# The sample's cross-attention scores of two heads, issued together in two column groups

## The reference

```python
def cross_attention(x, mem_k, mem_v, wq, wo):
    B, T, _ = x.shape
    q = (x @ wq).reshape(B, T, MEM_HEADS, MEM_HEAD_DIM)        # 4 heads of 512
    k = mem_k.reshape(B, -1, MEM_HEADS, MEM_HEAD_DIM)
    v = mem_v.reshape(B, -1, MEM_HEADS, MEM_HEAD_DIM)
    s = jnp.einsum('bqhd,bkhd->bhqk', q, k).astype(F32) * (MEM_HEAD_DIM ** -0.5)
    p = jax.nn.softmax(s, axis=-1).astype(x.dtype)
    o = jnp.einsum('bhqk,bkhd->bqhd', p, v).reshape(B, T, D_MODEL)
    return o @ wo
```

## Time and profile before

| | |
|---|---|
| time, median of 3 runs | 3115.37 us (3115.36 to 3124.46) |
| span of the profiled execution, first to last instruction | 3119.3 us; the page gives no other time of it |
| PE busy | 3036.5 us, 97% |
| DVE busy | 1907.7 us, 61% |
| ACT busy | 413.1 us, 13% |
| mean granted clock of TensorE | 0.987 |
| cross-attention stage, layer 0, layer 1 | 57.68 us, 56.70 us |

### The profile page before, as it was taken

The page is one execution under the profiler, slowest core; times in us unless marked ns, Lnnn a source line. Parts: engine busy times, 40 slices in busy tenths (PEclk is TensorE's granted clock), DMA queues, the critical chain, the costliest instruction groups (busy, mean ns, idle before and its releaser), DMA issues.

```text
span 3119.3 us, 47921 instructions
## 1 busy us (share of the span) xinstructions
PE 3036.5 (97%) x20530; PEld 2862.2 (92%) x20530; DVE 1907.7 (61%) x1485; ACT 413.1 (13%) x763; POOL 92.4 (3%) x64
## 2 busy tenths in 40 slices
PE   8999999899999999999999998999999999999998
PEld 6888899689989899999999996898999999999997
DVE  5666667646635766555565668744676555566565
ACT  2000003310220211000110003311031100011001
POOL 0000000100000000000000001000000000000000
PEclk9999999889999999999999999999999999999999
DMA  6666654234344355555555552453445555555542
GB/s 240 223 218 212 225 179 109 99 111 158 126 144 135 120 163 161 164 168 166 162 161 162 161 166 78 152 162 122 148 135 161 163 167 167 161 163 162 163 160 71
DMA packets 432693, 489.03 MB, mean 157 GB/s; under 512 B 16802, under 2 KB 388280, under 8 KB 431224
## 3 DMA queue, kind: packets, MB, share of 16 engines
q1 hardware_dynamic: 421344, 453.01, 46.0%
q0 software_dynamic: 4432, 18.15, 1.7%
q10 hardware_dynamic: 6836, 16.73, 1.5%
HBM read 476.47 MB, written 11.40 MB: 156 GB/s over the span
## 4 chain that ended last, share of the span: by engine, by line
PE 90%; DVE 7%; ACT 1%; DMA 1%; issue 1%; DVEq 0%; ACTq 0%
PE ps L217 24%; PE ps L219 24%; PE ps L218 24%; PE ps L370 4%; PE ps L371 4%; PE ps L372 4%; DVE WL L1336 2%; DVE X L1575 1%; PE ps L433 1%; PE ps L713 1%; PE ps L689 1%; DVE XL L1570 1%; DVE WH L1334 1%; PE ps L585 1%; PE ps L680 0%
## 5 line engine op out<-in xcount | busy, mean ns | idle before, releaser
L217 PE MATMUL ps<-XH,WH 128*128 128x288 f32 x3760 | 1117.3, 297 | 27.6 <-DVE XL L1341 11.8
L219 PE MATMUL ps<-XH,WL 128*128 128x288 f32 x3760 | 1111.5, 296 | 0.0
L218 PE MATMUL ps<-XL,WH 128*128 128x288 f32 x3760 | 1111.0, 295 | 0.0
L1334 DVE CAST WH<-RAW 128x2048 fp32r<-128x2048 f32 x433 | 535.5, 1237 | 837.6 <-PE ps L219 718.3
L1336 DVE TENSOR_TENSOR WL<-RAW,WH 128x2048 fp32r<-128x2048 f32 x433 | 1020.8, 2358 | 14.9
L217 PEld LDWEIGHTS ps<-XH,WH 128*128 128x128 f32 x3760 | 708.1, 188 | 37.0 <-issue 16.7
L218 PEld LDWEIGHTS ps<-XL,WH 128*128 128x128 f32 x3760 | 708.3, 188 | 0.2
L219 PEld LDWEIGHTS ps<-XH,WL 128*128 128x128 f32 x3760 | 708.3, 188 | 0.0
L217 PE MATMUL ps<-HH,WH 128*128 128x288 f32 x2048 | 604.7, 295 | 1.7 <-DVE WL L1336 1.7
L219 PE MATMUL ps<-HH,WL 128*128 128x288 f32 x2048 | 604.3, 295 | 0.0
L218 PE MATMUL ps<-HL,WH 128*128 128x288 f32 x2048 | 603.9, 295 | 0.0
(11 more groups left out here) (252 smaller groups left out, 1514.1 us busy)
## 6 DMA issues: line engine op xcount, KB each, us to landing
RAW<-in_mlp_up SPq DMA_DIRECT2D x128, 1024.0 KB, 5.4
RAW<-in_mlp_down SPq DMA_DIRECT2D x128, 1024.0 KB, 5.3
RAW<-in_xa_wk SPq DMA_DIRECT2D x32, 1024.0 KB, 5.1
RAW<-in_xa_wv SPq DMA_DIRECT2D x32, 1024.0 KB, 5.1
RAW<-in_xa_wq SPq DMA_DIRECT2D x32, 1024.0 KB, 5.4
RAW<-in_xa_wo SPq DMA_DIRECT2D x32, 1024.0 KB, 5.3
RAW<-in_w_in SPq DMA_DIRECT2D x22, 1024.0 KB, 5.3
RAW<-in_w_out SPq DMA_DIRECT2D x16, 1024.0 KB, 5.3
```

Source lines behind the costliest of these rows:

```text
L217: nc.tensor.matmul(out, wh, xh, start=start, stop=False)
L218: nc.tensor.matmul(out, wh, xl, start=False, stop=False)
L219: return nc.tensor.matmul(out, wl, xh, start=False, stop=stop)
L1334: V.tensor_copy(WH[:, h, :], RAW[:, s, :]).then_inc(split_hi, 1)
```

## The change

The sample's scores are no longer issued in each `scores(h)`. `scores(1)` issues those of heads 0 and 1, and `scores(3)` those of heads 2 and 3: for each of the four contraction tiles first the matmul of the one head, then that of the other, so that the column group alternates. ACT's copy of head 2's first key tile waits for scores(1), where it waited for scores(0), since KT[0] is read later. Number and shape of the matmuls stay.

Beside this, 31 semaphore names of the input stage and of the mixer are merged into five counters. The counts to wait for become the old ones plus what stands ahead in the group.

```diff
+    SIGNALS = {
+        "dve_inputs": (("memT_low", 8), ("xT_low", 16), ("conv", 32), ("sp_abs", 1), ("sp_done", 1), ("rec_ratio", 1)),
...
+        "pe_latents": (("stateT", 1), ("swap", 2), ("k_mm", 7), ("v_mm", 7), ("cacheT", 1)),
+    }
+    SIGNAL_OF = {n: (group, sum(c for _, c in of[:at])) for group, of in SIGNALS.items()
+                 for at, (n, _) in enumerate(of)}
+
     def sem(name):
+        if name in SIGNAL_OF:
+            name = SIGNAL_OF[name][0]
...
     def reached(name, n):
 
+        if name in SIGNAL_OF:
+            return sem(name), n + SIGNAL_OF[name][1]
...
-        pe.wait_ge(sem("xT_low"), NK)
+        pe.wait_ge(*reached("xT_low", NK))
...
-                def sample():
+                if h % 2:
                     for k in range(4):
-                        last = nc.tensor.matmul(ps[32 * h:32 * h + 32, 6, 0:256], QX[:, 4 * h + k, TP:T],
-                                                kt[:, k, 256:512], start=k == 0, stop=k == 3)
-                    return last
-
-                sample_last = sample()
+                        for hh in (h - 1, h):
+                            last = nc.tensor.matmul(ps[32 * hh:32 * hh + 32, 6, 0:256], QX[:, 4 * hh + k, TP:T],
+                                                    KT[hh % 2][:, k, 256:512], start=k == 0, stop=k == 3)
                 if h == 3:
-                    sample_last.then_inc(sem(f"{x}_s"), 1)
+                    last.then_inc(sem(f"{x}_s"), 1)
...
-                A(XH[:, k, :], ps[:, 4 + k % 4, 0:T], ACT.Copy).then_inc(sem("xT_high"), 1)
+                A(XH[:, k, :], ps[:, 4 + k % 4, 0:T], ACT.Copy)
...
                     if h >= 2 and k == 0:
-                        act.wait_ge(*reached(f"{x}_s", h - 1))
+                        act.wait_ge(*reached(f"{x}_s", 2))
```

More of the change, by code:

```diff
@@ L176, in build @@
     KIND_OF = {n: kind for kind, (names, _) in KINDS.items() for n in names}
+    SIGNALS = {
+        "dve_inputs": (("memT_low", 8), ("xT_low", 16), ("conv", 32), ("sp_abs", 1), ("sp_done", 1), ("rec_ratio", 1)),
+        "dve_latents": (("cq_n", 4), ("cq_low", 1), ("scanned", 1), ("ck_zero", 1), ("ck_n", 4), ("ck_low", 1),
+                        ("roped", 3)),
+        "act_gates": (("sp_exp", 1), ("cq_out0", 1), ("gates_sig", 16), ("tanh", 8), ("decay", 8), ("cq_out1", 1),
+                      ("sq_q", 1), ("rec_root", 1), ("ckv_out", 1)),
+        "pe_inputs": (("memT", 8), ("parT", 1), ("xT", 16), ("gate_mm", 16)),
+        "pe_latents": (("stateT", 1), ("swap", 2), ("k_mm", 7), ("v_mm", 7), ("cacheT", 1)),
+    }
+    SIGNAL_OF = {n: (group, sum(c for _, c in of[:at])) for group, of in SIGNALS.items()
+                 for at, (n, _) in enumerate(of)}
     def sem(name):
+        if name in SIGNAL_OF:
+            name = SIGNAL_OF[name][0]
         which, _, what = name.rpartition("_")
@@ L323, in mem_tiles @@
                 if r >= 4:
-                    pe.wait_ge(sem("memT_low"), r - 3)
+                    pe.wait_ge(*reached("memT_low", r - 3))
                 for k in range(2):
@@ L330, in mem_tiles @@
             pe.wait_ge(sem("par_in"), 16 * 12)
-            pe.wait_ge(sem("memT_low"), 8)
+            pe.wait_ge(*reached("memT_low", 8))
             for t, rows in enumerate((96, 96, 118)):
@@ L343, in x_tiles @@
                 if k >= 4:
-                    pe.wait_ge(sem("xT_low"), k - 3)
+                    pe.wait_ge(*reached("xT_low", k - 3))
                 for t, rows in enumerate((128, 128, 32)):
@@ L465, in _ @@
         pe.wait_ge(sem("gates_in"), 32)
-        pe.wait_ge(sem("conv"), 4 * LT)
+        pe.wait_ge(*reached("conv", 4 * LT))
         for n in range(2 * LT):
             if n >= 4:
-                pe.wait_ge(sem("gates_sig"), n - 3)
+                pe.wait_ge(*reached("gates_sig", n - 3))
             nc.tensor.matmul(ps[:, 4 + n % 4, 0:CW], GW[:, n, :], UC[:, n % LT, 0:CW], start=True,
@@ L473, in _ @@
         c0 = PHASES["ckv"]
-        pe.wait_ge(sem("cq_out0"), 1)
+        pe.wait_ge(*reached("cq_out0", 1))
         for q in range(2):
@@ L478, in _ @@
                       q == 0, q == 1).then_inc(chunk_used, 1)
-        pe.wait_ge(sem("gates_sig"), 2 * LT)
+        pe.wait_ge(*reached("gates_sig", 2 * LT))
         pe.wait_ge(sem("ones"), 1)
-        pe.wait_ge(sem("sq_q"), 1)
+        pe.wait_ge(*reached("sq_q", 1))
         for k in range(4):
@@ L486, in _ @@
         c0 = PHASES["kpe"]
-        pe.wait_ge(sem("cq_out1"), 1)
+        pe.wait_ge(*reached("cq_out1", 1))
         pe.wait_ge(chunk_split, c0 + 1)
@@ L505, in _ @@
         c0 = PHASES["uq"]
-        pe.wait_ge(sem("cq_low"), 1)
+        pe.wait_ge(*reached("cq_low", 1))
         pe.wait_ge(sem("kpe_out"), 1)
@@ L538, in _ @@
         pe.wait_ge(chunk_split, c0 + 1)
-        pe.wait_ge(sem("ck_low"), 1)
+        pe.wait_ge(*reached("ck_low", 1))
         for n in range(HEADS):
@@ L565, in _ @@
         pe.wait_ge(sem("v_out"), 8)
-        pe.wait_ge(sem("roped"), 3)
+        pe.wait_ge(*reached("roped", 3))
         for t, (c, rows) in enumerate(((0, 128), (128, 128), (384, 32))):
@@ L856, in _ @@
         for r in range(8):
-            act.wait_ge(sem("memT"), r + 1)
+            act.wait_ge(*reached("memT", r + 1))
             A(MTH[:, 2 * r:2 * r + 2, :].rearrange("p k n -> p (k n)"), ps[:, 4 + r % 4, :], ACT.Copy
               ).then_inc(sem("memT_high"), 1)
-        act.wait_ge(sem("parT"), 1)
+        act.wait_ge(*reached("parT", 1))
         for t, (n, c) in enumerate(((96, 0), (96, 96), (118, 192))):
@@ L911, in _ @@
         for n in range(2 * LT):
-            act.wait_ge(sem("gate_mm"), n + 1)
+            act.wait_ge(*reached("gate_mm", n + 1))
             m = n % LT
@@ L915, in _ @@
               bias=col((P_GAB if n < LT else P_GXB) + m)).then_inc(sem("gates_sig"), 1)
-        act.wait_ge(sem("gates_sig"), 2 * LT)
-        act.wait_ge(sem("sp_done"), 1)
+        act.wait_ge(*reached("gates_sig", 2 * LT))
+        act.wait_ge(*reached("sp_done", 1))
         act.wait_ge(sem("state_cols"), 2)
@@ L927, in _ @@
         A(CQ[:, 2:4, :], ps[:, 2:4, 0:T], ACT.Copy).then_inc(sem("cq_out1"), 1)
-        act.wait_ge(sem("cq_out0"), 1)
-        act.wait_ge(sem("cq_out1"), 1)
+        act.wait_ge(*reached("cq_out0", 1))
+        act.wait_ge(*reached("cq_out1", 1))
         A(SQM[:, :, :], CQ[:, :, :], ACT.Square).then_inc(sem("sq_q"), 1)
-        act.wait_ge(sem("rec_ratio"), 1)
+        act.wait_ge(*reached("rec_ratio", 1))
         A(TT[:, :, :], TT[:, :, :], ACT.Sqrt).then_inc(sem("rec_root"), 1)
@@ L960, in _ @@
         act.wait_ge(sem("pastT_out"), 2)
-        act.wait_ge(sem("ck_n"), 4)
+        act.wait_ge(*reached("ck_n", 4))
         A(CKH[:, :, :], CKT[:, :, :], ACT.Copy).then_inc(sem("ck_high"), 1)
@@ L968, in _ @@
         queries_out(3)
-        act.wait_ge(sem("stateT"), 1)
+        act.wait_ge(*reached("stateT", 1))
         A(SMALL[0:64, 128:256], ps[0:64, 7, 0:P], ACT.Copy).then_inc(sem("stateT_out"), 1)
@@ L976, in _ @@
             act.dma_start(dst, SMALL[r:r + n, 128:256]).then_inc(sem("stored"), 16)
-        act.wait_ge(sem("scanned"), 1)
+        act.wait_ge(*reached("scanned", 1))
         for n in range(HEADS):
             if n < HEADS - 1:
-                act.wait_ge(sem("k_mm"), n + 1)
+                act.wait_ge(*reached("k_mm", n + 1))
             else:
@@ L985, in _ @@
             if n < 7:
-                act.wait_ge(sem("v_mm"), n + 1)
+                act.wait_ge(*reached("v_mm", n + 1))
             else:
@@ L1212, in _ @@
         G.memset(RMS_EPS_COL, RMS_EPS).then_inc(sem("ones"), 1)
-        pool.wait_ge(sem("xT"), NK)
+        pool.wait_ge(*reached("xT", NK))
         pool.wait_ge(sem("par_done"), 1)
@@ L1401, in _ @@
         split(PHASES["cq"], 4)
-        dve.wait_ge(sem("decay"), LT)
+        dve.wait_ge(*reached("decay", LT))
         dve.wait_ge(sem("gated"), 1)
@@ L1430, in _ @@
         last.then_inc(sem("scanned"), 1)
-        dve.wait_ge(sem("scanned"), 1)
+        dve.wait_ge(*reached("scanned", 1))
         V.memset(CKT[:, :, KEYS:512], 0.0).then_inc(sem("ck_zero"), 1)
@@ L1445, in _ @@
         dve.wait_ge(sem("tables_in"), 16)
-        dve.wait_ge(sem("swap"), 2)
+        dve.wait_ge(*reached("swap", 2))
         bc = lambda x, n: x.unsqueeze(1).broadcast_to([P, n, T])
```

24 lines of the change are left out of this document (12 added, 12 removed).

## The result

The changed kernel takes 3126.39 us (median of 20 runs, 3122.94 to 3127.05), the kernel before 3116.82 us (20 runs, 3113.71 to 3130.7). The ratio, worked out from all runs of both, is 1.0023 (some 7 us), with a 95% interval of 1.0015 to 1.003; the two medians lie 9.6 us apart. So the change makes the kernel slower, where 3107.5 us and a range of 3103 to 3115 us were predicted. The 0.3% bound of the prediction (9.3 us) isn't crossed by the ratio, the range is missed by 11 us.

The account below looks back on a forecast made before the run. PE was taken as the bound, busy 97% of the span. Per layer 3.98 - 2 x 0.015 = 3.95 us, twice 7.9 us, off the median of 3115.37 us gave 3107.5 us; range 3103 to 3115 us.

Parts of the forecast that it names:

- The 0.3% bound of the prediction: Whole kernel: a measurement can tell about 0.3%, 9.3 us, from no change.
- Part 1: Cross-attention stages: removing the sample groups of heads 0 and 2 with their shape changes saves 3.98 us a layer.
- rival A: Sample scores in scores(1) and scores(3): no overlap, only shape changes saved, 1.0 us, 3114.4 us; chance 0.08.
- Part 2: Doubled sample groups in scores(1) and scores(3): each costs what a single one does, +0.015 us, reasoned from L723.
- The middle value: Doubled sample group: if every record had to start in the order of the code, it costs +0.22 us.
- Part 3: Cross-attention stages, who waits now: the stricter wait costs nothing, other waits keep slack, the sooner start is passed through.
- (a) to (e): Cross-attention: ACT's key copy, head 0's softmax, key and value loads, the tail, and wo's chunks; none takes back the gain.
- the tail keeps its form: Stage end from 929 us: waits of 0.89 and 1.82 us are measured from scores(3), neither swallowing nor adding.
- Part 4: Merged semaphores: the same instruction releases each wait; cost 0, with 0.2 us allowed in either direction.
- The last lines of the prediction: Signs of being wrong, among them a difference in front of 889 us from the merged counters; no size given.
- Rival C: Both cross-attention stages: the clock falls, six stretches at half clock give 3117.6 us; chance 0.06, 0.03 beyond 0.3%.
- The clock in the stages: Cross-attention stages: one half-clock stretch costs 1.7 us; which layer meets one was left open, -1.7 to +1.7 us.

Follow-up runs that it names:

- the one-group kernel: Score change head by head, both heads of a pair writing the second's column group, against the kernel before: 3115.68 us against 3117.45, ratio 0.9991.
- the repaired kernel: Changed kernel with waits for count 0 of merged signals kept at 0: 3107.63 us, ratio 0.997 to the kernel before; a second time 3108.47 us.
- the kernel with the filled wait: Kernel before plus PE's wait for all eight decay signals at cq's second block, ten unread matmuls ahead of it: 3124.74 us, ratio 1.0018.

## Why the prediction was wrong

- What bounds the kernel, and that PE's time in the attention stage counts in full: right. The scores alone give 7.5 us by the medians of the same comparison, and the two stages give 7.8 us in the profile.
- Part 1, the cost of a group and of the changes of shape: right, 3.88 us for a layer against 3.95. The small rest is head 0's, whose removal gives 1.89 + 3.65 - 3.69 = 1.85 us in the chain and not 1.93. Without overlap (the one-group kernel) some 0.9 us of gain is left by the chain, near the 1.0 us of rival A.
- Part 2, +0.015 us for the doubled group: right in size (1.92 and 1.85 us against 1.91 and 1.84). The reasoning from L723 was right for that row and too wide as a rule: there each head has only four records, no more than went ahead here without holding the other head back. Written head by head with eight records the pair takes 2.81 us. The middle value, +0.22 for an order that PE keeps strictly, has no case. The rule of the Trainium skill that matmuls start in program order ("TensorE: Matmul & The Clock Gate", section The mechanism) doesn't describe this chip's rows, in which the ninth record of the code starts with the fifth. The same section of the Trainium skill has the other rule, that a weight load overlaps only across row groups; it would have made 16 records dearer by 16 loads, and they take 1.92 us.
- Part 3, the waits (a) to (e): right; no new wait came. That the tail keeps its form held but for the clock: in layer 0 a wait of 1.82 us became 0.22 behind a weighted sum at half clock.
- **Part 4 failed.** "Each threshold is the old count plus all that precedes it there, so the same instruction releases each wait" is true for counts from 1 on. A wait for 0 was released by nothing, and after the shift something releases it. I had compared the lists of waits by name, where cq_out0 turned into act_gates and looked like a renaming, and not the counts. The price, put at 0 and at most 0.2 us in either direction, is 17 to 19 us by the medians and 17.8 by the profile: 13.1 us of gaps and 4.6 us of half clock behind them.
- The last lines of the prediction had named the sign, "a difference in front of 889 us, which the merged counters alone could bring", and given it no rival and no chance. Rival C, slower by the clock in the attention stages, was the wrong place: in the attention stages only one short stretch in each layer ran at half clock.
- The clock in the stages: the half clock stopped costing 1.7 us in layer 0's tail and began to cost them in layer 1's (L727 at 2143.60 takes 5.38 us in the chain). Both lie within the 1.7 us either way that were allowed; that they cancel is luck. The paragraph left out the stretch that moves the runs by most, the one in the MLA part, which I quoted for rival C and didn't price as scatter.

With the count-0 waits left free the prediction's sum comes out: 8.1 and 9.0 us under before by the medians, 3107.6 and 3108.5 us, against 7.9 and 3107.5.

## What to carry to other kernels

When semaphores are merged, list every wait with its count: a wait for 0 is free only on a counter of its own, and a loop whose first pass waits for its own count 0 is where it hides. Price an edit that "does nothing" by what it costs if that is wrong; here the cover was a count that nobody had to reach. An "issue" gap ahead of a wait on a shared counter can be a wait: look for what ended just before it on the engine that raises the counter. And matmuls of 32 columns pay when other column groups run beside them: alternate them, or leave no more than two float32 matmuls of one group in a row.

## What the runs showed of the hardware

- Two column groups of 32, alternating: 16 float32 records of 256 columns in 1.92 us, where the same 16 in one group need 3.64 us.
- PE starts records of another column group ahead of the order of the code: 1.94 us with four records of a group in a row, 2.81 us with eight. The rows fit a limit of three records in line behind the running one of the busy group; this is inferred from these two orders and from L723, and nothing else was tried.
- Between matmuls of 128 and of 32 columns PE loses 0.12 us on entry and 0.20 us on leaving. The changed kernel agrees for the second: L703 takes 3.65 us behind the sample's scores and 3.45 behind L727.
- An idle time of 9 us on PE was followed by 6 us of work at a granted clock of 0.50, the 1.2 GHz level; with PE kept busy over such a time ahead of the same work the clock stayed at 1.00. In the MLA part three matmuls ahead took away the 20.5 us at half clock of the repaired kernel, although PE is busy there in either case (20.50 of 20.50 us, 42.80 of 43.60). Without them the stretch lasted 20.5 to 51.2 us in all profiles but one, that of the kernel with the filled wait. Why the clock, once half, stays so in that part for such different times wasn't tried.
